# The picked experts' rows in two tables: two gathers of 512 KB where there was one of 1 MB

## What is computed

```python
    def block(args):
        xb, ib, gb = args
        act = jax.nn.gelu(jnp.einsum('td,thkd->thk', xb, u_tab[ib]), approximate=False)
        return jnp.einsum('thk,thkd->td', gb * act, v_tab[ib])
```

## Time and profile before

| | |
|---|---|
| median of 3 runs | 2218.09 us (2217.55 to 2221.16) |
| the profiled execution | 2222.17 us |
| its span | 2220.3 us |
| PE, DVE, ACT, POOL busy | 90%, 62%, 45%, 47% of the span |
| moved | 534.39 MB, of them 275.96 MB by the queue of POOL |
| the gathers | 256, issued from 421.19 us to 1048.16 us |

### The profile page before, as it was taken

How to read it: one execution, slowest core, us unless ns; L and a number is a source line. 1 busy time by engine, 2 the same in 40 slices (tenths; PEclk the granted TensorE clock), 3 DMA queues, 4 the chain that set the end, 5 groups by cost and what they waited for, 6 DMA issues and landing times.

```text
span 2220.3 us, 27167 instructions
## 1 busy us (share of the span) xinstructions
PE 2007.3 (90%) x9672; PEld 1476.8 (67%) x9672; DVE 1369.2 (62%) x2766; ACT 1001.0 (45%) x1829; POOL 1042.7 (47%) x840
## 2 busy tenths in 40 slices
PE   8998988987787877787999999999989999999998
PEld 1776666943233333333599777889978987778997
DVE  2767775496666676665457753277753775326776
ACT  1532344331212122212445687455554568845555
POOL 2362557764444444443387757800028865692000
PEclk9999999999989989989999999999999999999999
DMA  9242566599999999999655454555545534455553
GB/s 349 68 138 81 204 231 212 205 407 421 421 421 422 420 422 421 421 421 422 227 178 170 143 162 152 180 171 187 184 133 188 173 132 150 156 182 172 192 182 107
DMA packets 111446, 534.39 MB, mean 241 GB/s; under 512 B 12496, under 2 KB 12880, under 8 KB 77904
## 3 DMA queue, kind: packets, MB, share of 16 engines
q1 hardware_dynamic: 67104, 244.72, 33.3%
q0 software_dynamic: 38720, 275.96, 30.3%
q10 hardware_dynamic: 5488, 11.98, 1.7%
HBM read 531.49 MB, written 1.11 MB: 240 GB/s over the span
## 4 chain that ended last, share of the span: by engine, by line
PE 59%; DMA 22%; DVE 7%; ACT 7%; issue 3%; POOL 2%; ACTq 0%; DVEq 0%; SPq 0%; POOLq 0%
PE psum L867 57%; DMA pair_rows<-in_peer_uv,arena 10%; DMA arena<-in_peer_uv,arena 7%; DMA wring<-in_peer_uv,arena 3%; ACT w_hi L1410 2%; PE psum L924 1%; POOL w_lo L2765 1%; ACT arena L1421 1%; POOL w_lo L2763 1%; DMA wring<-in_w_ada 1%; ACT arena L1750 1%; DVE arena L2505 1%; ACT arena L1695 0%; DVE arena L2521 0%; DMA wring<-in_w_in_hy 0%
## 5 line engine op out<-in xcount | busy, mean ns | idle before, releaser
L2763 POOL TENSOR_TENSOR w_lo<-wring,w_hi 128x512 fp32r<-128x512 f32 x280 | 377.1, 1347 | 573.1 <-ACT w_hi L1410 567.1
L1410 ACT ACTIVATE w_hi<-wring 128x1024 fp32r<-128x1024 f32 (+1 forms) x414 | 434.3, 1054 | 330.1 <-PE psum L867 305.0
L867 PE MATMUL psum<-w_hi,a_hi 128*128 128x512 f32 (+1 forms) x1056 | 423.4, 401 | 30.6 <-POOL w_lo L2765 14.4
L867 PE MATMUL psum<-w_lo,a_hi 128*128 128x512 f32 (+1 forms) x1056 | 412.0, 390 | 0.0
L867 PE MATMUL psum<-arena 128*128 128x512 f32 (+7 forms) x1142 | 353.2, 465 | 64.2 <-ACT arena L1624 46.6
L867 PE MATMUL psum<-w_hi,a_lo 128*128 128x512 f32 (+1 forms) x1056 | 411.2, 389 | 0.0
L2765 POOL TENSOR_TENSOR w_lo<-wring,w_hi 128x512 fp32r<-128x512 f32 x280 | 394.3, 1408 | 0.0
L867 PE MATMUL psum<-a_hi,w_hi 128*128 128x256 f32 x1312 | 376.6, 287 | 5.0 <-DVE a_lo L1892 3.4
L867 PE MATMUL psum<-a_hi,w_lo 128*128 128x256 f32 x1312 | 372.1, 284 | 0.0
L867 PE MATMUL psum<-a_lo,w_hi 128*128 128x256 f32 x1312 | 372.0, 284 | 0.0
L867 PEld LDWEIGHTS psum<-arena 128*128 128x128 f32 (+2 forms) x1142 | 189.9, 203 | 208.6 <-issue 133.8
(11 more groups left out here) (261 smaller groups left out, 2397.6 us busy)
## 6 DMA issues: line engine op xcount, KB each, us to landing
wring<-in_w_up SPq DMA_DIRECT2D x88, 512.0 KB, 3.5
wring<-in_w_xbc SPq DMA_DIRECT2D x48, 512.0 KB, 3.4
wring<-in_w_dn SPq DMA_DIRECT2D x44, 512.0 KB, 3.3
wring<-in_w_adaT SPq DMA_DIRECT2D x32, 512.0 KB, 4.3
wring<-in_w_qkv SPq DMA_DIRECT2D x32, 512.0 KB, 3.6
wring<-in_w_z SPq DMA_DIRECT2D x32, 512.0 KB, 3.4
wring<-in_w_g SPq DMA_DIRECT2D x32, 512.0 KB, 3.4
wring<-in_w_ps SPq DMA_DIRECT2D x32, 512.0 KB, 3.3
```

The lines of the kernel that those rows point to most:

```text
L867: mm = lambda o, a, b, start, stop: nc.tensor.matmul(o, a, b, start=start, stop=stop, skip_group_check=True)
L1410: a.reaches(A(w_hi[:, n % SPLIT_RING, 0:width], wring[:, c % RING, 0:width], ACT.Copy), hi_ready, n + 1)
L2763: nc.gpsimd.tensor_tensor(w_lo[:, r, 0:half], wring[:, c % RING, 0:half], w_hi[:, r, 0:half].bitcast(F32), ALU.subtract)
```

## The change

The two tables stay apart, and each pick is gathered by two indirect transfers, of 128 rows of 4 KB each. The first brings the down rows into the first half of the place, with the semaphore `pair_in`; the second brings the up rows into the second half, with a semaphore `values_in` of its own for each place. DVE still waits for `pair_in`. PE waits for `values_in` as well as for the diagonal matrix. The places, their order, what frees them, and the order of the picks are as before.

```diff
@@ -213,7 +213,7 @@
-    o["peer_uv"] = np.concatenate([i["peer_u"][0], i["peer_v"][0]], 1)
+    o["peer_u"], o["peer_v"] = i["peer_u"][0], i["peer_v"][0]
@@ -1204,6 +1204,7 @@
                     if n == PICKS - 4:
                         pe.wait_ge(S("first_scaled"), 1)
                         tile_turned("L0.", 0)
+                    pe.wait_ge(S(f"values_in{place_of(n)}"), 16 * place_turn(n))
                     pe.wait_ge(S("diag_ready"), n + 1)
@@ -2803,9 +2804,12 @@
             if place_before(n) is not None:
                 pool.wait_ge(S("pair_used"), place_before(n) + 1)
-            pool.indirect_dma_start(out=pair(n), out_offset=None, in_=d["peer_uv"],
+            pool.indirect_dma_start(out=pair(n)[:, 0:D], out_offset=None, in_=d["peer_u"],
                                     in_offset=bass.IndirectOffsetOnAxis(ap=pidx[:, g, j:j + 1], axis=0)
                                     ).then_inc(S(f"pair_in{place_of(n)}"), 16)
+            pool.indirect_dma_start(out=pair(n)[:, D:2 * D], out_offset=None, in_=d["peer_v"],
+                                    in_offset=bass.IndirectOffsetOnAxis(ap=pidx[:, g, j:j + 1], axis=0)
+                                    ).then_inc(S(f"values_in{place_of(n)}"), 16)
```

## The result

| | before | after |
|---|---|---|
| median | 2218.94 us (2217.55 to 2221.16, 4 runs) | 2252.90 us (2250.24 to 2260.71, 4 runs) |
| ratio, 95% interval | | 1.015 [1.0125, 1.0175] |
| profiled execution | 2222.17 us | 2254.21 us |
| its span | 2220.3 us | 2252.3 us |
| last dot begins | 1077.58 us | 1110.22 us |

The change costs 34 us, 1.5%. The forecast was 70 us. In the profiled executions the loss is 32.0 us, and the last dot begins 32.6 us later. So all of it arises up to the end of the stage of the gathers, as forecast. The dot of pick 31 already comes 14.9 us later than before (525.49 us, 510.64), and the other 224 picks add 17.8.

The account below looks back on a forecast made before the run. The prediction took POOL's issue as the new bound, replacing the DMA engines: pick 7 at 449.1 plus 248 x 2.80 us, landing at 1148.0, puts the last dot 70.4 us later, so the median becomes 2288.5 us, range 2235 to 2332.

Parts of the forecast that it names:

- The start: Before the gather stage: six extra issues delay chunk 15's low part 7.4 us; pick 7 goes out at 449.1, 5.3 us later.
- The undisturbed issue and its floor: POOL in the gather stage: 0.94 us per gather plus a 0.30 us gap, twice per pick, 2.48 us.
- That a gather started inside a dot is held to its end: POOL beside DVE: a gather starting inside a running dot waits for its end; such gathers averaged 1.34 us, others 0.95.
- The landing on idle engines: Gather stage: with almost idle engines, down rows land about 4.55 us after their issue, and the dot starts then.
- The engines' pace: DMA engines in the gather stage: 2.49 us per pick with rows of 4 KB, as with 8 KB rows.
- The bounds of 2.49 to 2.82: DMA engines in the gather stage: us per pick with 4 KB rows, from weight chunks at 421 and 372 GB/s.
- The 2.80 us per pick: POOL's pace from pick 7 over 248 picks: issue floor 2.48 us plus holds by dots, 2.71 to 2.83, taken as 2.80.
- what I count at nothing is the queue of ten gathers: it drains: Gather stage: the DMA queue empties at no cost; time from issue to landing drops from 26 to about 5 us.
- The hold of 0.23 to 0.35 us per pick: POOL in the gather stage: every fourth gather start falls inside a dot and waits, adding this to 2.48 us per pick.
- POOL is the bound at 2.60 to 2.97: Gather stage, the forecast case: POOL's issue sets 2.60 to 2.97 us per pick, 2239 to 2331 us; chance 0.70.
- Rows of 4 KB slow the engines: Gather stage rival: engines need 2.82 us per pick, POOL goes on waiting for places, 2290 to 2300 us; chance 0.04.
- POOL keeps up: Gather stage rival: starts fall clear of dots or issue is hidden; 2.48 to 2.55 us per pick, 2214 to 2227; chance 0.13.

Follow-up runs that it names:

- experiment 3: The changed kernel with picks 0 to 6 gathered whole from the joint table as before: 2250.09 us, ratio 1.0146.
- experiment 6: The changed kernel with only 512 of 1024 columns of the up rows gathered and the dots' tokens in PSUM: 2221.33 us, ratio 1.0006 to the kernel before.
- experiment 5: The changed kernel with the dots' second operand, the tokens, in PSUM for all picks but the last four, nothing left out: 2241.59 us, ratio 1.0089.
- experiments 2: The changed kernel with only 512 of the 1024 columns of the up rows gathered, TensorE taking the same 512 twice: 2327.65 us, ratio 1.0481.
- experiments 1: The changed kernel with each dot over only 128 of the 1024 columns: 2243.92 us, ratio 1.0100.
- experiment 8: The changed kernel with tokens in PSUM and each pick split into rows of 7.5 KB and 0.5 KB (1920 and 128 columns): 2246.74 us, ratio 1.0114.
- experiment 7: The changed kernel with the two gathers of a pick in the other order, up rows first: 2250.51 us, ratio 1.0143.
- the 960 columns: The changed kernel with 960 of the 1024 columns of the up rows gathered, TensorE's work per pick unchanged: 2289.34 us, ratio 1.0310.

## Why the prediction was right in sign and wrong in size

The time lay inside the range and the sign was right; the loss was half of what was forecast. By its own steps:

- **The start: right to 0.5 us, but by luck.** Pick 7 was forecast at 449.1 us and came at 449.58. The low part of chunk 15 ended at 444.6 us and not at 445.7 (the first gather went out 1.0 us earlier than before). The query product behind it then took 4.7 us and not 2.88. TensorE had stood idle 1.7 us before it began, as before the product of chunk 14, and from 445.1 to 448.4 us its granted clock was 0.50, the level of 1.2 GHz; its matmuls came each 0.21 us where they come each 0.12 at 2.4 GHz. The two errors cancel. (The three products of 8.63 us are those of chunks 13 to 15: the first copy in the earlier trace rows is that of chunk 12.) What the start is worth is less sure: with it undone the last gather of down rows went out only 1.8 us earlier (experiment 3).
- **The undisturbed issue and its floor: right.** 0.94 + 0.30 us for a gather with half the bytes, so 2.48 us per pick; experiment 6 runs at 2.504. The Trainium skill's sentence that the time to start a DMA is usually small beside the DMA ("DMA: Bandwidth & Descriptors", section "Issuing engines are not separate DMA queues") does not hold for these gathers: 1.24 us beside 1.28 of transfer.
- **That a gather started inside a dot is held to its end: right,** and experiment 5 shows by what. It costs 11 us of the 34.
- **The landing on idle engines: right as a number** (forecast 4.55 us, first gather of down rows 4.5), **wrong as the value for the steady stage,** which is 6.6. Even where the engines aren't full it is 5.2 to 5.4 (experiments 2 and 6).
- **The engines' pace: too low.** I took 2.49 us for rows of 4 KB, because six us of weight chunks ran at 421 GB/s. It is 2.56 (409 GB/s, experiments 1, 5 and 8). The bounds of 2.49 to 2.82 held it. The estimate of 2.57 that the prediction worked out from the 408.7 GB/s of the Trainium skill (same page, section "iDMA fabric — 4 AXI ports for 8 engines, asymmetric across TPBs") was right on the number, and I set it aside because it lay "still below POOL's". That page measured a load stream in rows of 4 KiB, not pairs of gathers, so the match may be chance. It is also a warning on windows: the earlier trace rows held large transfers only, and the price sits in the second transfer, not in the row length (experiment 8). By itself this error does not explain the forecast, which was too high.
- **The 2.80 us per pick, through "what I count at nothing is the queue of ten gathers: it drains": the step that failed.** The hold of 0.23 to 0.35 us per pick, and from it the 2.80, followed from a dot 4.55 us after its issue, with engines that need less than POOL. (The mean of the old gathers, 1.089 us, gave 2.78 beside it; it is 1.01 now.) In the changed kernel the dot starts 6.65 or 7.90 us after its issue, another gather is the held one, and the same model then gives 0.08 us of hold and 2.56 per pick, the engines' pace. Measured 2.63 per pick over the stage: 248 x (2.80 - 2.6285) = 42.5 us of the forecast are not there. The later start (+0.5) and the last landing (8.8 in place of 4.55 us, +4.2) give back 4.7: 1148.0 - 42.5 + 4.7 = 1110.2, where the last dot is.

Against before, the 34 us are experiment 5's +22.6, and 11 us of held gathers. Of the 22.6 an estimate gives the engines' ceiling (2.56 - 2.49) x 248 = 17 us, and the start the other 5; the start was never tried alone in that kernel. The held gathers aren't spread evenly. The dot of pick 31 comes 7.2 us later in the changed kernel than in experiment 5 (525.49 and 518.30 us), and the 224 picks behind it add 2.6: the larger part falls in the first picks, where dots stand close. Picks 127 to 175 are slower too. DVE finishes the first tile before the dot of pick 144, which comes 4.4 us after the one before, and the next dots stand close (1.6 us), but with the up rows first (experiment 7) the picks from 151 to 175 take 2.58 after the same delay, so what sets off that stretch isn't settled.

So none of the prediction's cases was the true one. "POOL is the bound at 2.60 to 2.97" has the number, but not the cause: its own test said engines at 0.89 of full and 375 GB/s. "Rows of 4 KB slow the engines" has the full DMA share and the lower rate, but at a quarter of its price, and without POOL waiting for places. "POOL keeps up" has the shift of the dots' phase, which is what happened, but not to where all starts are clear, and its 2.48 to 2.55 per pick are below the engines' 2.56. That the sign and the range came out right owes something to this: a loss was forecast from one bound and arose mostly from the other. The two paces lay 0.08 us apart, and then they are not rivals: each works on the other.

## What to carry to other kernels

- Splitting a gather costs the issuing engine the whole issue again (1.24 us, for rows of 0.5 to 8 KB alike) and the DMA engines a little (0.07 us per pick). Work out both paces before the split; where both come near the old one, a loss is likely.
- Where two paces are within a few per cent, do not price one with the other's queue gone. Ask which of them keeps a queue; less work on that side can make the kernel slower, as the 960 columns did.
- A forecast that adds up right may hold two errors. Check its parts against the trace, as with the start here.
- If GpSimd's issue is the bound and VectorE reads two operands from SBUF beside it, put one of them in PSUM: 11 us here, 106 us in experiment 6, and nothing where the issue had slack.

## What the runs showed of the hardware

- A gather of 128 rows holds GpSimd for 0.94 us with rows of 2, 3, 4 and 8 KB alike, and for up to 2.0 us where it starts in a dot with two operands in SBUF. The dot isn't lengthened by more than some hundredths (1.23 us, at most 1.30).
- Two gathers per pick reach 409 GB/s, one 421, with the same bytes; neither the row length nor the number of recorded packets (11 or 18 per engine) changes the 409.
- A DMA share over 100% with a landing of 6.6 us and an issuing engine that never waits for a place are possible together. A full share does not say that the engines are the only bound, nor how near they are to their best rate (98.6% at 369 GB/s, 91.9% at 315): 20.3 us of landing in experiment 5 showed what they look like when they are.
- With a deep queue one of the 16 parts of every transfer falls behind the others (up to 8.7 us in the kernel before), and the dots wait for it: 2.53 us per pick where the bytes say 2.49.
